# Delta rule steps in even units, group norm in other slots, full transposes for v and b/k, four-tile products, four banks for the mixing units

## The reference, cut to what matters

```python
h = rms_norm(x, norm1_g); proj = h @ w_in          # columns for A, attention, pooling, gates
p = p + (token_shift(p) - p) * mu                  # mixer A: "mixing"
r, k, v = ...; xw, xa, xg = ...
decay = exp(-exp(-softplus(-(w0 + tanh(xw) @ w_up)) - 0.5)); a = sigmoid(a0 + xa @ a_up)
kk = normalised heads(k * k_k);  k = k * (1 + (a - 1) * k_a)
def step(S, (r_t, w_t, k_t, v_t, a_t, b_t)):       # a_t = -kk, b_t = kk * a
    sa = S @ a_t
    S = S * w_t + outer(sa, b_t) + outer(v_t, k_t)
    return S, S @ r_t
o = group_norm(o per head) * lnx_g + lnx_b; y = (o + bonus * v) * sigmoid(xg) @ g_up
# then attention, pooling, three gated branches, w_out, residual, squared-ReLU MLP
```

## Time and profile before

| what | value |
|---|---|
| median of 3 runs (lowest, highest) | 481.9 us (479.48, 483.32) |
| the profiled execution: its time, its span | 482.88 us, 481.1 us |
| PE, DVE, ACT, POOL busy | 97%, 62%, 51%, 7% |
| chain that ended last | PE 82%, ACT 5%, DVE 5%, DMA 3% |
| mean granted clock of PE | 0.993 of full |

### The profile page before, as it was taken

The page is one execution under the profiler, slowest core; times in us unless marked ns, Lnnn a source line. Parts: engine busy times, 40 slices in busy tenths (PEclk is TensorE's granted clock), DMA queues, the critical chain, the costliest instruction groups (busy, mean ns, idle before and its releaser), DMA issues.

```text
span 481.1 us, 8816 instructions
## 1 busy us (share of the span) xinstructions
PE 468.5 (97%) x3696; PEld 403.6 (84%) x3696; DVE 296.3 (62%) x405; ACT 247.0 (51%) x371; POOL 33.1 (7%) x41
## 2 busy tenths in 40 slices
PE   7999999999998998999999999999999999999997
PEld 4989987878986776787888888999999999999995
DVE  4666798754555556576668867655555555555542
ACT  6569564445547444675643445654444445444530
POOL 2000100020672000102000000000000000000000
PEclk9999999999999999999999999999999999999999
DMA  8887635353434333246466465575665655666602
GB/s 237 220 227 218 198 103 162 89 163 103 132 91 113 107 90 89 89 129 216 131 219 192 142 182 173 171 219 174 189 204 183 198 188 181 185 200 181 194 25 87
DMA packets 74294, 76.91 MB, mean 160 GB/s; under 512 B 2576, under 2 KB 54544, under 8 KB 74256
## 3 DMA queue, kind: packets, MB, share of 16 engines
q1 hardware_dynamic: 74256, 76.36, 52.8%
HBM read 75.30 MB, written 1.05 MB: 159 GB/s over the span
## 4 chain that ended last, share of the span: by engine, by line
PE 82%; ACT 5%; DVE 5%; DMA 3%; issue 2%; SPq 1%; ACTq 0%; DVEq 0%
PE bank L492 24%; PE bank L494 24%; PE bank L493 24%; DMA stage<-in_w_in 3%; ACT w_hi L898 2%; DVE w_lo L1137 2%; PE bank L735 1%; PE bank L757 1%; PE bank L620 1%; PE bank L746 1%; DVE small L1348 1%; DVE h_lo L1159 1%; PE bank L719 1%; DVE att L1341 1%; DVE xs L1454 1%
## 5 line engine op out<-in xcount | busy, mean ns | idle before, releaser
L1137 DVE TENSOR_TENSOR w_lo<-stage,w_hi 128x1024 fp32r<-128x1024 f32 x138 | 168.8, 1228 | 122.2 <-ACT w_hi L898 121.9
L898 ACT CAST w_hi<-stage 128x1024 fp32r<-128x1024 f32 x138 | 144.3, 1051 | 116.0 <-PE bank L494 95.6
L492 PE MATMUL bank<-h_hi,w_hi 128*128 128x256 f32 x384 | 110.5, 288 | 0.7 <-DVE big L1395 0.4
L494 PE MATMUL bank<-h_hi,w_lo 128*128 128x256 f32 x384 | 109.3, 285 | 0.0
L493 PE MATMUL bank<-h_lo,w_hi 128*128 128x256 f32 x384 | 109.3, 285 | 0.0
L492 PEld LDWEIGHTS bank<-h_hi,w_hi 128*128 128x128 f32 x384 | 74.1, 193 | 2.3 <-issue 1.4
L493 PEld LDWEIGHTS bank<-h_lo,w_hi 128*128 128x128 f32 x384 | 74.2, 193 | 0.7
L494 PEld LDWEIGHTS bank<-h_hi,w_lo 128*128 128x128 f32 x384 | 74.2, 193 | 0.0
L492 PE MATMUL bank<-w_hi,h_hi 128*128 128x512 f32 x144 | 61.2, 425 | 0.0
L494 PE MATMUL bank<-w_hi,h_lo 128*128 128x512 f32 x144 | 56.9, 395 | 0.0
L493 PE MATMUL bank<-w_lo,h_hi 128*128 128x512 f32 x144 | 56.8, 395 | 0.0
(11 more groups left out here) (228 smaller groups left out, 530.3 us busy)
## 6 DMA issues: line engine op xcount, KB each, us to landing
stage<-in_w_ff SPq DMA_DIRECT2D x64, 512.0 KB, 4.1
stage<-in_w_in SPq DMA_DIRECT2D x54, 512.0 KB, 3.9
stage<-in_w_branch SPq DMA_DIRECT2D x12, 512.0 KB, 4.6
stage<-in_w_out SPq DMA_DIRECT2D x8, 512.0 KB, 4.1
xs<-in_x SPq DMA_DIRECT2D x2, 512.0 KB, 3.9
out<-xs SPq DMA_DIRECT2D x4, 256.0 KB, 2.1
cst<-in_consts SPq DMA_DIRECT2D x1, 608.0 KB, 6.1
att<-in_w SPq DMA_DIRECT2D x1, 256.0 KB, 5.1
```

The source lines that it names most:

```text
L492: pe.matmul(o, lh, rh, start=first, stop=False)
L494: return pe.matmul(o, ll, rh, start=False, stop=last)
L898: nc.scalar.copy(w_hi[:, v % RING], stage[:, v % STAGES]).then_inc(hi_done, 1)
L1137: dve.tensor_tensor(w_lo[:, v % RING], stage[:, v % STAGES], w_hi[:, v % RING].bitcast(F32), ALU.subtract)\
```

## The change

1. The steps: `STEP_AT` puts step n at unit 16 + 2n; step 0 at parts 1, 2, 3 as before, steps 1 to 3 at parts 0, 1, 2. Of the last level's transposes chunk pair 1 moves from (16, 0) to (17, 0).
2. Group norm: mean at (19, 3) and (23, 2), variance at (20, 3) and (24, 1), scaling at (21, 3) and (25, 1), the turn of o at (22, 3) and (25, 3).
3. v, and b with k, are turned by full 128 x 128 transposes; ACT's copies out of PSUM are then by halves. ACT's copies `swapped` (L963) are gone.
4. Each product of 64 x 128 weights becomes two of 64 x 64, on all four quarters of the array.
5. The feat units use banks 0, 1, 2, 3, 0, 1, 0 (then 1, 0). The decay's addition goes ahead of unit 2's `low` pieces on DVE, and ACT's part of it ahead of one cast.

```diff
-S_STEP, STEPS = 16, 4
-S_NORM, S_GN = (19, 23), (21, 25)
+STEPS = 4
+STEP_AT = {(16 + 2 * n, i + (n == 0)): (n, work) for n in range(STEPS) for i, work in enumerate(("U", "sa", "o"))}
+LAST_XT_AT = {(16, 0): 0, (17, 0): 1}
+MEAN_AT = {(19, 3): 0, (23, 2): 1}
+VAR_AT = {(20, 3): 0, (24, 1): 1}
+ROOT_AT = {(21, 3): 0, (25, 1): 1}
+S_GN = (22, 25)
+FEAT_BANK = {0: 0, 1: 1, 2: 2, 3: 3, 4: 0, 5: 1, 6: 0, 13: 1, 14: 0}
...
-                    use(("unit", t), t % 2, dense=True)
+                    use(("unit", t), FEAT_BANK[t], dense=True)
...
-                    pe.wait_ge(swapped, c + 1)
...
-                        ins = pe.matmul(o[:, P * i:P * i + P], bk[c][halves[e], j, s, HD * e:HD * e + P],
+                        ins = pe.matmul(o[halves[e], P * i:P * i + P], bk[c][halves[e], j, s, 0:HD],
+                                        ar[c][halves[e], j, :, HD * s:HD * s + HD], start=True, stop=True)
+                    for e, o in enumerate(both):
+                        ins = pe.matmul(o[halves[1 - e], P * i:P * i + P], bk[c][halves[e], j, s, HD:P],
...
+                        o = room(pe, ("vt", c))
+                        for j in range(PAIRS):
+                            ins = pe.transpose(o[:, P * j:P * j + P], vmix[:, j, P * c:P * c + P], ident)
+                        ins.then_inc(full_of(("vt", c)), 1)
...
+                    for s in range(2 - c):
+                        o = room(pe, ("bk", c, s))
+                        for j in range(PAIRS):
+                            ins = pe.transpose(o[:, P * j:P * j + P], bk[c][:, j, s], ident)
+                        ins.then_inc(full_of(("bk", c, s)), 1)
...
+                        turned = take(act, ("bk", c, s))[:].rearrange("p (j e n) -> p j e n", j=PAIRS, e=2)
+                        nc.scalar.copy(bkt[c][:, 0, s], turned[:, :, 0])
+                        for i in range(2):
+                            ins = nc.scalar.copy(bkt[c][halves[1 - i], 1, s], turned[halves[i], :, 1])
...
-                if t in S_NORM:
-                    c = S_NORM.index(t)
-                    if p == 0:
-                        act.wait_ge(oc_ready, c + 1)
-                        nc.scalar.activation(osq, oc[c], ACT.Square).then_inc(osq_ready, 1)
+                if (t, p) in MEAN_AT:
+                    c = MEAN_AT[t, p]
+                    act.wait_ge(oc_ready, c + 1)
+                    nc.scalar.activation(osq, oc[c], ACT.Square).then_inc(osq_ready, 1)
```

More of the change, by code:

```diff
@@ L189, in pe_uses @@
     if (t, p) == (7, 3):
-        return [(("vt", c, e),) for c in range(TT) for e in range(2)]
+        return [(("vt", c),) for c in range(TT)]
     out = []
@@ L200, in pe_uses @@
     if (t, p) in BK_AT:
-        out += [(("bk", BK_AT[t, p], e),) for e in range(2)]
+        out += [(("bk", BK_AT[t, p], s),) for s in range(2 - BK_AT[t, p])]
     l = level_place(t)
     if l is not None:
-        if p == 0 and l < LEVELS:
+        if p == 0:
             out += [(("Y", l, e),) for e in range(2)]
@@ L713, in extra @@
                     c = BK_AT[t, p]
[L714 to L722 removed]
+                    for s in range(2 - c):
+                        o = room(pe, ("bk", c, s))
+                        for j in range(PAIRS):
+                            ins = pe.transpose(o[:, P * j:P * j + P], bk[c][:, j, s], ident)
+                        ins.then_inc(full_of(("bk", c, s)), 1)
                 l = level_place(t)
[L724 removed]
+                if l is not None and p == 0:
                     if l == 0:
@@ L805, in extra @@
                 if work == "o" and n < STEPS - 1:
-                    for e in range(2):
-                        copied(pe, ("bk", c, e))
+                    copied(pe, ("bk", c, s))
                     o = room(pe, ("dS", n))
@@ L955, in extra @@
                     for c in range(TT):
-                        for e in range(2):
-                            o, rows = take(act, ("vt", c, e)), halves[1 - e]
-                            nc.scalar.copy(zz[c][rows, :, :, e], o[rows].rearrange("p (s j n) -> p s j n", s=2, j=PAIRS))\
-                              .then_inc(drained_of(("vt", c, e)), 1)
-                if (t, p) in ((7, 1), (8, 0)):
-                    c = t - 7
-                    act.wait_ge(b_ready, c + 1)
-                    nc.scalar.copy(bk[c][HD:P, :, :, P:P + HD], bk[c][HD:P, :, :, 0:HD]).then_inc(swapped, 1)
+                        turned = take(act, ("vt", c))[:].rearrange("p (j e n) -> p j e n", j=PAIRS, e=2)
+                        for s in range(2):
+                            for e in range(2):
+                                ins = nc.scalar.copy(zz[c][halves[1 - e], s, :, e], turned[halves[s], :, e])
+                        ins.then_inc(drained_of(("vt", c)), 1)
                 if (t, p) == (7, 2):
+                    copied(act, ("kb", 0))
                     act.wait_ge(zero_ready, 2)
@@ L982, in extra @@
                         o = take(act, ("XT", l - 1, c))
-                        if l < LEVELS:
-                            ins = nc.scalar.copy(xt_c[c].rearrange("p j e n -> p (j e n)"), o[:])
-                        else:
-                            turned = o[:].rearrange("p (j e n) -> p j e n", j=PAIRS, e=2)
-                            for s in range(2):
-                                for e in range(2):
-                                    ins = nc.scalar.copy(xt_f[c][halves[e], s], turned[halves[s], :, e])
-                        ins.then_inc(drained_of(("XT", l - 1, c)), 1)
-                if l is not None and p == 2 and l < LEVELS:
+                        nc.scalar.copy(xt_c[c].rearrange("p j e n -> p (j e n)"), o[:]).then_inc(drained_of(("XT", l - 1, c)), 1)
+                if (t, p) in LAST_XT_AT:
+                    c = LAST_XT_AT[t, p]
+                    o = take(act, ("XT", LEVELS - 1, c))
+                    turned = o[:].rearrange("p (j e n) -> p j e n", j=PAIRS, e=2)
+                    for s in range(2):
+                        for e in range(2):
+                            ins = nc.scalar.copy(xt_f[c][halves[e], s], turned[halves[s], :, e])
+                    ins.then_inc(drained_of(("XT", LEVELS - 1, c)), 1)
+                if l is not None and p == 2:
                     for s in range(2):
@@ L1271, in extra @@
                 l = level_place(t)
-                if l is not None and p == 0 and l < LEVELS:
+                if l is not None and p == 0:
                     for e in range(2):
@@ L1483, in _ @@
                 inverse_norm(n)
-            for e in range(2):
-                copied(pool, ("bk", 0, e))
+            for s in range(2):
+                copied(pool, ("bk", 0, s))
             pool.memset(pu[:, :, 0:PAD], 0.0).then_inc(pad_ready, 1)
```

116 lines of the change are left out of this document (51 added, 65 removed).

## The result

The changed kernel takes **483.5 us** (median of 20 runs, 482.1 to 485.8), the kernel before 482.1 us in the runs beside it (20 runs, 479.5 to 484.2). The ratio is 1.0036, with a 95% interval of 1.0020 to 1.0052: 1.7 us slower by the ratio (1.4 by the medians), where 1.2 us faster was forecast, and 0.5 us outside the range of 8 in 10. Two later sets of runs gave 1.0052 (1.0031 to 1.0073) and 1.0062 (1.0036 to 1.0088). The profiled execution has a span of 482.6 us and a time of 484.4, so the two profiles differ by 1.5 us.

The account below looks back on a forecast made before the run. PE, busy 97% of the span, was taken as the bound. Terms -3.3 + 0 + 0.3 + 0.4 + 0.8 + 0.6 + 0 = -1.2 us gave 480.7 us against the median 481.9; 8 in 10 within 476.8 to 483.0.

Parts of the forecast that it names:

- Turning v and b/k: Full transposes of v and b/k instead of 64 x 64 matmuls: less PE work, -3.3 us.
- Products: 32 matmuls of 64 x 64 weights replace 16 of 64 x 128 per call: 0 us, bounds -0.2 and +0.6 a call.
- The start: Early decay delays piece 11, so PE waits 2.3 us before the norms of k: +0.3 us, bounds -0.4 and +0.6.
- Behind b/k's turn: One more ACT copy ahead of the cast, low and masking that level 0 waits for: +0.4 us, at least 0.
- The steps: Delta-rule waits in units 16, 18, 20, 22, 5.4 us against 4.6: +0.8; three more small-work places: +0.6 us.
- The clock: Half-clock stretches of PE, priced at 1.4 us each: one goes, one comes, 0 us in sum.
- The one at 155 goes with its wait: Half-clock stretch at 155 us goes as unit 16's wait falls to 0.7; unit 20's 3.2 us should bring another.
- The one at 46 stays: Half-clock stretch at 46 us, at the start, stays because the norms and a wait are still ahead of it.
- Rival 3: At the start, 2.3 us idling and the norms bring the half clock earlier and longer: +1.7, 482.4 us; chance 0.12.
- I am wrong if: Signs against it: unit 20's wait under 1.5 us, norms of k before 42 us, or a PE wait at an unnamed place.

Follow-up runs that it names:

- e2: The kernel before with the early decay (decay sums and sigmoids moved ahead) alone: 483.4 us, 1.0057 of the kernel before.
- e10: The changed kernel with steps and group norm back in the units of before: 481.3 us, 0.9975 of the kernel before.
- e7: The changed kernel with ACT's sigmoids back in the old order, DVE's decay sums still early: 481.8 us, 1.0024 of the kernel before.
- e11: The changed kernel run again, unedited, on the chip of e10: 484.1 us, 1.0052 of the kernel before.
- e3: The kernel before with the mixing (feat) units on four banks instead of two, nothing else: 481.7 us, 1.0005 of the kernel before.
- e6: The kernel before with the full transposes, the layout of bk and the four-tile products alone: 478.2 us, 0.9942 of the kernel before.
- e13: e6 with the mixing (feat) units on four banks instead of two: 478.3 us, 0.9936 of the kernel before.
- e1: The changed kernel with the decay order of before on DVE and ACT: 481.4 us, 0.9999 of the kernel before.
- e17: The changed kernel with 22 useless matmuls in each of two PE waits (norms of k, unit 20): 481.3 us, 1.0005 of the kernel before.

## Why the prediction was wrong, step by step

**Turning v and b/k: right.** Forecast -3.3 (its parts, -1.2, -1.1, -0.6 and -0.3, add to -3.2); 3.45 by the starts of v's turn and of level 0, with the four calls of the products in it. v's eight transposes take 72.69 - 71.86 = 0.83 us.

**Products: right,** 0 forecast. A call takes 1.04 us, before 1.09, so the four give 0.2. The rule of the Trainium skill (TensorE: Matmul & The Clock Gate, "Measured speedup vs the span model"), by which I estimated 0.95 us for a call, errs by 0.09 and my 1.09 by 0.05; the measurement decides. Two numbers of the prediction's paragraph don't come out. "Twice the columns gives 27 ns" is not twice the level's 17, which would be 34; it is 107 over four tiles, and no row is named for the 107 (the eight transposes of the earlier trace rows, at 128 columns each, take some 100). The new trace has four matmuls every 0.11 us, 27 ns each, so the number was right by another way than the one given. And by the skill's rule, with half of 107 for 64 columns, the level's matmuls come to 16 ns and not 14 to 15, nearer to the 17 measured than I had made it.

**The start: wrong,** +0.3 forecast. The step that failed is "Piece 11, by my estimate, lands 4.8 us later". It was issued at 33.9 and not 33.8, and landed 5.7 us later, outside all the loads in the earlier trace rows, so 39.6 and not 38.6. From its cast to the end of the square it took just the 3.47 us forecast (40.64 to 44.11). So the norms were 1.3 us later instead of 0.3. In e2 they were 1.5 later, and PE waited 3.3 us for them there and 3.4 in e10. I had taken a value between the median and the most of the loads around. But the most, 5.0, was this very piece, issued at 32.6 in the trace of before: the load at this place is never the median one. In the eleven other profiles with DVE's sums late it took 4.8 to 5.4 us, in the seven with both parts early 5.4 to 6.0, in e7 5.0. Why it takes longer behind the early sums, no run shows. (By the same sum the lower bound, landing in 3.8, should be -0.7 and not -0.4.)

**Behind b/k's turn: right in place, 0.3 too small** (0.7 for 0.4).

**The steps: right.** Waits forecast 0.7, 0.7, 3.2 and 0.6; measured 0.77 in unit 16, 0.6 in unit 18, 2.96 in unit 20 and 0.7 in unit 22 (0.3 for the copy of U and 0.4 before o). Together 5.0 against 4.6 before, so +0.4 where +0.8 was forecast. The chain mean, square, cast, `low`, copy of U is in the trace as it was worked out. Without the clock the steps and their three more entries cost 1.4 to 2.3 us (e10, e11), and 1.3 between the two profiles, each of which has one half-clock stretch there; the forecast was 1.4. What an entry costs by itself no run shows.

**The clock: wrong,** 0 forecast, and this is the larger part of the miss. Two steps failed. "The one at 155 goes with its wait (0.7 left); the 3.2 us in unit 20 should bring one of its own": both happened in the profile, but this sets a stretch that comes in some executions against one that comes in most. The stretch at 155 is in the profiles of the kernel before, e3 and e10. It is not in those of e2, e6 and e13, which have the same wait there; the one in unit 20 is in five profiles of six with its wait. What I had read from two stretches of one trace, 1.2 us of idling at 190 and 1.8 before 155, was no rule. In e2:

```profile
154.40:158.00 3.60, 2.16 (x22) 1.59 (x22) 1.81 (x3) 0.86 (x2) 0.00 (x0) 1.00 0.39 100
```

The kernel before loses 1.5 to 2.9 us to the clock on average, the changed kernel 4.4 to 5.2. The other step is "The one at 46 stays": it took one stretch for the most that the start could bring, and the profile has two, from 44.6 us on, which cost the 1.58 us between the norms and v's turn. Rival 3 (0.12) had this right, with 1.7 us; but it was weighed against a wait of 2.3 us, and the wait was 3.0.

Between the two profiles the account closes without any of unit 20's clock, since one stretch stands there for another: the forecast was -1.2 and they differ by +1.5, a miss of 2.7, of which the landing of piece 11 is 1.0, the second stretch at the start 1.6 and level 0 0.3, less small gains.

The terms as the runs give them, in us of the whole: turning -2.8 (e6), early decay +1.8 to +2.7 (e1, e2), steps and norm +2.8 to +3.7 (e11 against e10), banks 0. The sum is +1.8 to +3.6, the measured 1.7 to 3.0. With the clock set apart, the terms are about -2.5, +1.1 and +1.4 to +2.3, near 0 or a little over; the clock makes most of the difference. What stays open is how the price of the early decay divides between DVE and ACT.

None of the three signs in "I am wrong if" came up: the wait in unit 20 was 2.96 us, the norms started at 44.16, and PE had no new wait at a place that the prediction doesn't name. They tested where the waits would be, and that was right; neither the size of the wait at the norms nor the clock over many executions was among them.

## What to carry to other kernels

Price an idle stretch of PE twice, once as a wait and once by what it does to the clock, and take the second from many executions and not from one profile: a single trace can show a half-clock stretch that comes in some executions only. When work is moved ahead in a queue that also frees buffers, the load behind it moves too, and may land later than the median of the others. Before steps are spread over more units, look for the one operation that stands ahead of the copy that is waited for; here two small moves took 3 us of waiting away, where the rearrangement added 0.4.

## What the runs showed of the hardware

Useless matmuls in two waits made the kernel 3.3 us faster (484.6 to 481.3; 2.7 by the ratios), since the clock stayed at its full level: mean clock 0.996 to 1.000 in all 12 executions, against 0.985 to 0.993 in 12 of the same kernel without them.

The time of one kernel spreads by up to 6 us, much of it with the granted clock of the execution. Of the 23 executions of the kernel before beside e17, those at a mean clock of 0.999 or more took 479.1 to 481.8 us, those at 0.992 or 0.993 481.8 to 485.0. The mean clock moves in steps of about 0.0035, which is one stretch of 3.4 us at half speed in 480 (3.4 x 0.5 / 480).

The same two weight pieces of 512 KB (10 and 11, issued between 30.7 and 35.4 us) took 3.8 to 6.0 us from issue to landing in these kernels' profiles.
